# Weight sums of a block product: two of four made by accumulating loads, and the product's seven terms spread between other units

## What is computed

```python
def _swiglu(h, w_in, w_out):
    gu = h @ w_in
    gate, up = jnp.split(gu, 2, axis=-1)
    return (jax.nn.silu(gate) * up) @ w_out
...
    for l in range(DEPTH):
        x = x + 0.5 * _swiglu(_rmsnorm(x, ffn1_norm[l]), ffn1_w_in[l], ffn1_w_out[l])
        ...
        x = x + jnp.concatenate([out_a, out_b], axis=-1) @ w_mix_out[l]
        x = x + 0.5 * _swiglu(_rmsnorm(x, ffn2_norm[l]), ffn2_w_in[l], ffn2_w_out[l])
```

## Time and profile before

| what | us |
|---|---|
| median of 3 runs | 982.07 (978.37 to 983.84) |
| the profiled execution | 981.96 |
| its span, first to last instruction | 980.2 |
| TensorE busy | 902.0 |
| VectorE busy | 715.7 |
| ScalarE busy | 507.6 |

### The profile page before, as it was taken

How to read it: one execution, slowest core, us unless ns; L and a number is a source line. 1 busy time by engine, 2 the same in 40 slices (tenths; PEclk the granted TensorE clock), 3 DMA queues, 4 the chain that set the end, 5 groups by cost and what they waited for, 6 DMA issues and landing times.

```text
span 980.2 us, 10918 instructions
## 1 busy us (share of the span) xinstructions
PE 902.0 (92%) x4118; PEld 731.5 (75%) x4118; DVE 715.7 (73%) x857; ACT 507.6 (52%) x554; POOL 68.6 (7%) x123
## 2 busy tenths in 40 slices
...
GB/s 318 305 85 213 317 97 221 238 299 87 65 290 268 121 115 215 280 135 267 263 229 157 109 214 298 100 206 256 277 87 66 290 268 126 128 197 279 147 250 54
DMA packets 138467, 194.49 MB, mean 198 GB/s; under 512 B 9796, under 2 KB 94600, under 8 KB 138416
## 3 DMA queue, kind: packets, MB, share of 16 engines
q1 hardware_dynamic: 136432, 189.17, 58.2%
q0 software_dynamic: 1808, 4.49, 2.3%
...
...
## 4 chain that ended last, share of the span: by engine, by line
PE 40%; DVE 26%; DMA 17%; SPq 7%; ACT 6%; issue 3%; ACTq 0%; DVEq 0%
DVE w_lo L1093 13%; DMA h_rows<-qs 8%; DVE raw L1118 6%; DMA raw<-in_ffn_w_in_dram 5%; ACT w_hi L750 5%; PE U L1595 4%; PE U L1596 4%; PE U L1598 4%; SPq L470 4%; DMA gv<-h_rows 3%; PE C L1595 3%; PE C L1596 3%; PE C L1598 3%; PE TR L1595 3%; PE TR L1596 3%
## 5 line engine op out<-in xcount | busy, mean ns | idle before, releaser
L1093 DVE TENSOR_TENSOR w_lo<-raw,w_hi 128x2048 fp32r<-128x2048 f32 (+1 forms) x182 | 403.9, 2239 | 139.2 <-ACT w_hi L750 138.4
L750 ACT ACTIVATE w_hi<-raw 128x2048 fp32r<-128x2048 f32 (+1 forms) x178 | 333.2, 1891 | 208.0 <-DVE raw L1118 88.4
L1595 PE MATMUL U<-w_hi,xT 128*128 128x512 f32 (+1 forms) x352 | 137.6, 391 | 0.6 <-DVE xT L1261 0.6
L1596 PE MATMUL U<-w_lo,xT 128*128 128x512 f32 (+1 forms) x352 | 135.9, 386 | 0.0
L1598 PE MATMUL U<-w_hi,xT 128*128 128x512 f32 (+1 forms) x352 | 135.7, 386 | 0.0
L1595 PE MATMUL TR<-w_hi,xT 128*128 128x512 f32 x256 | 99.8, 390 | 0.0
L1598 PE MATMUL TR<-w_hi,xT 128*128 128x512 f32 x256 | 99.6, 389 | 0.0
L1596 PE MATMUL TR<-w_lo,xT 128*128 128x512 f32 x256 | 99.6, 389 | 0.0
L1595 PE MATMUL C<-w_hi,hT_hi 128*128 128x512 f32 x176 | 71.8, 408 | 15.0 <-DVE hT_lo L1175 15.0
L1595 PEld LDWEIGHTS U<-w_hi,xT 128*128 128x128 f32 x352 | 67.5, 192 | 14.3 <-DVE xT L1261 1.0
L1598 PEld LDWEIGHTS U<-w_hi,xT 128*128 128x128 f32 x352 | 67.5, 192 | 13.3
(11 more groups left out here) (206 smaller groups left out, 1269.5 us busy)
## 6 DMA issues: line engine op xcount, KB each, us to landing
raw<-in_ffn_w_in_dram SPq DMA_DIRECT2D x168, 512.0 KB, 6.3
raw<-in_ffn_w_out_dram SPq DMA_DIRECT2D x88, 512.0 KB, 6.3
raw<-in_w_mix_in_dram SPq DMA_DIRECT2D x28, 512.0 KB, 8.6
raw<-in_w_mix_out_dram SPq DMA_DIRECT2D x16, 512.0 KB, 4.0
...
xc<-bias_rows POOLq DMA_DIRECT2D x16, 192.0 KB, 6.4
```

The costliest lines, as they stand in the source:

```text
L750: return act.activation(w_hi[:, slot_of(u), cols], raw[:, raw_of(u), cols], ACT.Copy)
L1093: return dve.tensor_tensor(w_lo[:, slot_of(u), cols], raw[:, raw_of(u), cols], w_hi[:, slot_of(u), cols].bitcast(F32), ALU.subtract)
L1595: pe.matmul(out_, x_hi, w_hi[:, slot, c], start=start, stop=False, skip_group_check=reopened)
L1596: pe.matmul(out_, x_hi, w_lo[:, slot, c], start=False, stop=False, skip_group_check=reopened)
```

## The change

The seven terms are made and used in another order (B11, T1, T2, T3, B22, B21, T4), with units of `in` and `out` between them: `out` 1 or 4 and one unit of `in` c+2 come earlier, the pair's own `out`s later. T1 and T3 are no longer added by VectorE: GpSimd issues loads of B12 onto the slot that holds B11, and of B22 onto the slot of B12, that add to what is there (`accum_op`). VectorE keeps T2 and T4. B12 and B22 are still loaded plainly too. The trips of h, the banks and the raw slots follow the new order, and the end of the stage has `out` 7 and 8 around the transposes of chunk 10. ScalarE's order follows VectorE's and is left out below, as are the removed lists and the second pair's lines, which repeat the first's with 4 added to the chunks (`out` 4 in the place of `out` 1).

```diff
 OUT_TILES = (4, 6, 0, 2)
 QUADS = (3, 7)
 SINGLES = (0, 1, 2, 5, 6, 9, 10)
-TERMS = ("B11", "B21", "T1", "T2", "T3", "T4", "B22")
+TERMS = ("B11", "T1", "T2", "T3", "B22", "B21", "T4")
+FIRST_OUT = {3: 1, 7: 4}
 MIX = ("KV", "Q0", "Q1", "V0", "V1", "U0", "U1", "M0", "M1", "M2", "M3")
 LAYERS = 2
 
 
     def quad(c):
         term = {n: (s, "sum", c, n) for n in TERMS}
-        return [term["B11"], term["B21"], term["T1"], term["T2"], (s, "out", c - 1), term["T3"], term["T4"], term["B22"],
-                *inner(c + 2), (s, "out", c), (s, "out", c + 1), *inner(c + 3), (s, "out", c + 2)]
-
-    return [*inner(0), *inner(1), (s, "out", 0), *inner(2), (s, "out", 1), *quad(3), *quad(7), (s, "out", 10)]
+        return [term["B11"], (s, "out", FIRST_OUT[c]), term["T1"], (s, "in", c + 2, 0), term["T2"], (s, "out", c - 1), term["T3"],
+                (s, "in", c + 2, 1), term["B22"], term["B21"], term["T4"], (s, "in", c + 3, 0), (s, "out", c + 2),
+                (s, "in", c + 3, 1), (s, "out", c)]
+
+    return [*inner(0), *inner(1), (s, "out", 0), *inner(2), *quad(3), *quad(7), (s, "out", 8), (s, "out", 10)]
 
 
 def stage_used(s):
 
     made = stage_made(s)
-
-    def later(a, b):
-        made.remove(a)
-        made.insert(made.index(b) + 1, a)
-
     if s > 0:
-        later((s, "out", 0), (s, "in", 2, 0))
-    for c in QUADS:
-        later((s, "out", c - 1), (s, "sum", c, "T3"))
+        made.remove((s, "out", 0))
+        made.insert(made.index((s, "in", 2, 0)) + 1, (s, "out", 0))
     return made
 
...
     if u[1] != "sum":
         return [u]
-    return [(u[0], "sum", u[2], n) for n in ("B11", "B12", "B21", "B22")] if u[3] == "B11" else []
+    return [(u[0], "sum", u[2], n) for n in {"B11": ("B11",), "T1": ("B12",), "T2": ("B22",), "B21": ("B21",)}.get(u[3], ())]
 
 
...
 RAW_OF = {"B11": "B11", "B21": "B21", "B22": "B22", "T1": "B11", "T2": "B11", "T4": "B11", "T3": "B12"}
-HT_SLOT = {0: 0, 1: 1, 2: 0, 3: 0, 4: 1, 5: 0, 6: 1, 7: 0, 8: 1, 9: 1, 10: 0}
+HT_SLOT = {0: 0, 1: 1, 2: 0, 5: 1, 3: 0, 4: 1, 6: 0, 9: 1, 7: 0, 8: 1, 10: 0}
+HT_BEFORE = {5: 1, 6: 3, 9: 4, 3: 5, 7: 9}
 
 
...
     return [(c, t) for c in cs for t in range(2)]
 
 
-SILU_ORDER = counts(lambda s: [*both((0, 1, 2)), (3, 0), (3, 1), *both((5, 6)), (7, 0), (7, 1), *both((9, 10))])
-H_ORDER = counts(lambda s: [*both((0, 1, 2)), (3, 1), (3, 0), *both((5, 6)), (7, 1), (7, 0), *both((9, 10))])
+SILU_ORDER = counts(lambda s: both((0, 1, 2, 5, 3, 6, 9, 7, 10)))
+H_ORDER = SILU_ORDER
 HT_ORDER = H_ORDER
 HT_PSUM_ORDER = counts(lambda s: [(c, t) for c in (0, 10) if not by_trip(s, c) for t in range(2)])
-TRIP_ORDER = counts(lambda s: [(c,) for c in (0, 1, 2, 3, 5, 6, 7, 9) if by_trip(s, c)])
+TRIP_ORDER = counts(lambda s: [(c,) for c in (0, 1, 2, 5, 3, 6, 9, 7) if by_trip(s, c)])
 TRIP_B_ORDER = counts(lambda s: [(c,) for c in QUADS])
 GU_ORDER = counts(lambda s: [(c,) for c in SINGLES])
-ADD_ORDER = counts(lambda s: [(c, n) for c in QUADS for n in ("T1", "T3", "T2", "T4")])
+ADD_ORDER = counts(lambda s: [(c, n) for c in QUADS for n in ("T2", "T4")])
+SUM_LOAD_ORDER = counts(lambda s: [(c,) for c in QUADS])
 SNAP_ORDER = counts(lambda s: [(c, n) for c in QUADS for n in ("s1", "s2", "s3")])
-SUM_ORDER = counts(lambda s: [(c, n) for c in QUADS for n in ("gate0", "up1", "up0")])
+SUM_ORDER = counts(lambda s: [(c, n) for c in QUADS for n in ("up1", "up0", "gate0")])
 
 
...
 
     U = [bank("U0"), bank("U1")]
     TR = [bank("TR0"), bank("TR1")]
-    BANKS = {0: U, 1: TR, 2: U, 5: [TR[1], U[1]], 6: [U[0], TR[0]], 9: [TR[1], TR[0]], 10: U}
-    QUAD_BANKS = {3: (TR[0], TR[1], U[0]), 7: (U[1], TR[1], U[0])}
+    BANKS = {0: U, 1: TR, 2: U, 5: U, 6: [U[1], TR[1]], 9: [U[1], TR[1]], 10: [TR[1], U[0]]}
+    QUAD_BANKS = {3: (TR[0], U[0], TR[1]), 7: (TR[0], U[1], U[0])}
     acc = [[bank("C0"), bank("C1")], [bank("D0"), bank("D1")]]
...
+        load_block(s, 3, "B11")
         load_out(s, 1)
+        if by_trip(s, 0):
+            store_h(s, 0)
         load_block(s, 3, "B12")
         if by_trip(s, 0):
             load_h(s, 0)
+        load_in(s, 5, 0)
         store_h(s, 1)
         load_block(s, 3, "B22")
         load_h(s, 1)
         load_out(s, 2)
+        store_h(s, 2)
+        load_in(s, 5, 1)
+        load_h(s, 2)
+        load_block(s, 3, "B21")
+        load_in(s, 6, 0)
+        load_out(s, 5)
+        load_in(s, 6, 1)
+        load_out(s, 3)
+        store_h(s, 5)
+        load_block(s, 7, "B11")
+        load_h(s, 5)
+        load_out(s, 4)
+        store_g(s, 3)
+        load_block(s, 7, "B12")
+        store_h(s, 3)
+        load_g(s, 3)
+        load_h(s, 3)
+        load_in(s, 9, 0)
+        load_block(s, 7, "B22")
+        load_out(s, 6)
+        store_h(s, 6)
+        load_in(s, 9, 1)
+        load_h(s, 6)
+        load_block(s, 7, "B21")
+        load_in(s, 10, 0)
+        load_out(s, 9)
+        load_in(s, 10, 1)
+        load_out(s, 7)
+        store_h(s, 9)
+        load_out(s, 8)
+        load_h(s, 9)
+        load_out(s, 10)
+        store_g(s, 7)
+        store_h(s, 7)
+        load_g(s, 7)
+        load_h(s, 7)
+        if after is not None:
+            after()
 
     sp.dma_start(xs[:, 0, :], x_tiles[0]).then_inc(x_loaded[0], 16)
     load_first(0, 0)
...
         rsqrt(L, rstd[:, c0:c0 + groups], sums[:, c0:c0 + groups], mean[:, c0:c0 + groups], n,
               groups).then_inc(rstd_done, 1)
 
+    def add_block(s, c, to, name, landed_):
+
+        dst = raw[:, RAW_SLOT[s, "sum", c, to], :].rearrange("p (k n) -> p k n", k=4)
+        k0, col = 4 * (name[1] == "2"), DFF + c * FC
+        for i in range(2):
+            pool.dma_start(dst[:, 2 * i:2 * i + 2, :], w_in[s % 2][s // 2, :, k0 + 2 * i:k0 + 2 * i + 2, col:col + 2 * FC],
+                           accum_op=ALU.add).then_inc(landed_, 16)
+
+    def add_blocks(s, c):
+
+        r, n = landed((s, "sum", c, "B12"))
+        pool.wait_ge(unit_loaded[r], n)
+        add_block(s, c, "B12", "B22", T3_landed)
+        pool.wait_ge(lo_ready, n_made((s, "sum", c, "B11")))
+        add_block(s, c, "B11", "B12", T1_landed)
+
     inverse_rms(0, 0, 0)
     with nc.allow_non_contiguous_dma(reason="256 numbers, once"):
         pool.dma_start(rb[:, :], rel_bias.rearrange("b h -> h b")).then_inc(rb_loaded, 16)
...
     for j, u in enumerate([(s, "sum", 3, "B11"), (s, "sum", 3, "T2"), (s, "in", 5, 0), (s, "in", 6, 0)]):
         pool.wait_ge(units_used, n_used(u))
         pool.dma_start(ws[32 * j:32 * j + 32, :, :].rearrange("a g (i b) -> a (g i) b", b=32),
...
     if name[0] == "B":
         split(u)
         return
-    act.wait_ge(terms_added, ADD_ORDER[s, c, name])
+    if name == "T1":
+        act.wait_ge(T1_landed, 32 * SUM_LOAD_ORDER[s, c])
+    elif name == "T3":
+        act.wait_ge(T3_landed, 32 * SUM_LOAD_ORDER[s, c])
+    else:
+        act.wait_ge(terms_added, ADD_ORDER[s, c, name])
     hi_of(u).then_inc(hi_ready, 1)
 
...
             act.activation(s1, s1, ACT.Silu, scale=inv[:, 0:1]).then_inc(silu_done, 1)
         else:
             act.wait_ge(units_used, n_used((s, "sum", c, "T4")))
+            act.wait_ge(h_done, H_ORDER[s, c + 2, 1])
             act.activation(gate_pair, QUAD_BANKS[c][0][:, :], ACT.Silu, scale=inv[:, 1:2]).then_inc(silu_done, 1)
 
     def copy_sum(s, c, name):
...
+            act.wait_ge(units_used, n_used((s, "out", HT_BEFORE[c])))
         for kk in range(2):
             act.activation(h_as_tokens(hT_hi[:, HT_SLOT[c], kk, :]), h_as_loaded(h_cols, kk), ACT.Copy
                            ).then_inc(hT_hi_done, 1)
 
     def round_pair(s, c, t):
 
-        if t == 1:
+        if t == 0:
+            act.wait_ge(units_used, n_used((s, "out", HT_BEFORE[c])))
+            act.wait_ge(g_loaded, 64 * TRIP_B_ORDER[s, c])
+        else:
             act.wait_ge(h_loaded, 64 * TRIP_ORDER[s, c])
-        else:
-            act.wait_ge(g_loaded, 64 * TRIP_B_ORDER[s, c])
         act.activation(pair_as_tokens(hT_hi, t), pair_as_loaded(h_cols if t == 1 else g_cols), ACT.Copy
                        ).then_inc(hT_hi_done, 1)
...
 
     def add_term(s, c, name):
 
-        to, other = {"T1": ("B11", "B12"), "T2": ("B11", "B22"), "T3": ("B12", "B22"), "T4": ("B11", "B21")}[name]
+        to, other = {"T2": ("B11", "B22"), "T4": ("B11", "B21")}[name]
         r, n = landed((s, "sum", c, other))
         dve.wait_ge(unit_loaded[r], n)
-        if name == "T3":
-            r, n = landed((s, "sum", c, to))
-            dve.wait_ge(unit_loaded[r], n)
         a, b = [raw[:, RAW_SLOT[s, "sum", c, x_], :] for x_ in (to, other)]
         dve.tensor_tensor(a, a, b, ALU.add).then_inc(terms_added, 1)
 
...
+    combine_x(s)
+    term(3, "B11")
+    rest_h(s, 1)
     out(1)
+    rest_x(s)
+    multiply(s, 2, 0)
+    term(3, "T1")
+    add_term(s, 3, "T2")
+    multiply(s, 2, 1)
+    turn_h(s, 2)
+    made(5, 0)
+    term(3, "T2")
+    out(2)
+    rest_h(s, 2)
+    term(3, "T3")
+    add_term(s, 3, "T4")
+    made(5, 1)
+    term(3, "B22")
+    term(3, "B21")
```

(76 more changed lines are left out.)

224 lines of the change are left out of this document (92 added, 132 removed).

## The result

The changed kernel takes 1038.85 us in the median of 5 runs (1037.49 to 1044.71), against 982.07 before: a ratio of 1.0588 (95% interval 1.0549 to 1.0627), slower by 57 us. I had forecast 989 with a range to 1018. The chance for slower was 0.45, the largest of the three, but the size lies outside the range. The profiled execution took 1044.71 us, 5.9 above the median; its span is 1042.8 us and the mean granted clock 0.934 (0.963 before).

What follows compares the result with a forecast made beforehand. TensorE was taken to bound the kernel, with some 108 us lost to waits and slow clock. New losses of 90.4, 21 and 4 make 115.4 against 108, so +7: 989 us, range 955 to 1018.

Steps and rivals of the forecast that it cites:

- VectorE's sums: VectorE makes 16 sums fewer, 36.4 us less busy; time falls only where a wait is ordered behind them.
- The waits at out 5 and out 9: TensorE waits 4.1 us for rest_h at each, plus 1 us of slow clock, in every stage.
- No DMA can cure it: The out 5 and out 9 waits, in every stage, cannot be cured by any DMA.
- The end of the stage: Around the transposes of h: 0.5 us left a stage; the ends lose about 24 us now.
- Out 3: Second pair's T1 load lands late: 10.4 us wait, 1.5 of slow clock, a stage; clock counts from T3's product end.
- rival 1: Accumulating loads as cheap as plain ones: out 3 waits 3.7 us and 1 of slow clock, 960 us; chance 0.32.
- The rule of the Trainium skill: A DMA reduction is half as fast as a copy: two units 12.6 us, some 997 in all.
- The first pair: Waits at out 1 and in 5 with slow clock: 7 us in stages 1 to 3, 0 in stage 0.
- hidden but for this place: The 16.8 MB of added load traffic costs nothing except at out 3.
- Rival 2: Accumulating loads cost twice the software queue's price: 14.6 us more a stage, 1047 us; chance 0.13.
- Rival 3: VectorE runs far ahead, order-bound waits close; nearly all 108 us but first pair's and cheap out 3's go: about 930; chance 0.06.

Runs made afterwards that it cites:

- e8: e11 with the halves of out 1 and of T1 also put ahead of h of chunk 1; VectorE makes all four sums: 921.10 us.
- e12: e8 with T3 alone made by an accumulating load, issued once T1's sum has read B12: 922.69 us.
- e1: Changed kernel's new order, with VectorE making all sums and no GpSimd loads for the pairs: 993.38 us.
- e11: e1 with the first pair's rest_pair ahead of the second pair's T1 halves, and h of chunks 5 and 9 ahead of units queued in front: 946.92 us.
- e4: Changed kernel with round_pair and rest_pair of chunk 3 ahead of the second pair's T1 halves and T2 sum: 992.94 us.
- e3: Changed kernel with GpSimd's loads overwriting instead of adding, so T1 and T3 are B12 and B22 alone (a timing probe): 998.94 us.
- e2: Changed kernel with GpSimd issuing T1's accumulating load ahead of T3's: 1019.08 us.
- e9: e8's order with the changed kernel's accumulating loads, T1's issued first; T1's halves stay behind x_hi: 982.11 us.

## Why the prediction was wrong

**VectorE's sums: right.** It is 36.1 us less busy, and "no bound by throughput, only by order" holds: e8 has the work of before on VectorE and none of the waits for low halves of the earlier trace rows, and e12 has 8 sums fewer than e8 and is no faster.

**The waits at out 5 and out 9: right.** Forecast 4.1 us each, in every stage; the trace has 3.9 to 5.2 at the eight places, 4.11 at out 5 of stage 1. The clock after them costs more than the 1 us I gave (6.0 less 4.1 at out 5): behind the wait the starts lie up to 0.43 us apart until 417.4 us, where 1 us had stood for about five of them, and the granted clock of the stretch is 0.90. "No DMA can cure it" was right, too: L1231 is 38.2 us in e1, which has no such loads, against 40.0. What cured it was order (e11).

**The end of the stage: right.** No wait at the transposes is left in the table.

**Out 3: the mechanism was right and the size too small.** The step gave 11.9 us a stage; 18 are measured. T3's product ends at 388.16 us in TensorE's timeline of stage 1, so on the prediction's clock:

| step | forecast | measured |
|---|---|---|
| `turn_g(3)` ends | 17.2 | 18.7 |
| B12' landed | 24.3 | 27.3 |
| T1' landed | 38.3 | 44.3 |
| out 3 starts | 45.4 | 51.5 |

Each link is a little late. Landing took B12' 8.2 us and not 6.3; the DMA share of that stretch is 0.88, and that this is the reason is likely but not shown. From GpSimd's first issue to T1' there are 17.1 us and not 14: an addition costs 6.0 us a unit, not the 5.3 that I took from the nearest row, and GpSimd's issuing 1.2 us each (4.91 for four), not 0.6. e4 shows that this chain set the wait, since its move takes L1246 away.

Part of the nearness is luck. The 5.3 us a unit came from the other loads on the same queue and was taken for that queue's price, but plain loads of a unit cost 3.1 there (e3), the hardware queue's 3.16; it is the addition that makes 6.0. And at the plain price the step would have failed by more: rival 1 gave out 3 a loss of 4.7 us a stage, while e3, with that price, loses 11.7 there (12.5 in stage 0, 12.1 in stage 1).

The rule of the Trainium skill that I had weighed ("Collectives: The Full Stack", section "The bandwidth ceiling: the fold count and why AG ≠ RS ≠ AR"), half speed for a reduction, holds here in its number: 6.0 against 3.1 us a unit. Its reason, two reads for a sum, no run shows; the queue's packets are nearly twice as many with the addition. By it I had put 12.6 us for two units, near the 11.9 measured, but it would have moved the sum by 8 us only, to 997.

**The first pair: this step failed.** It said 7 us a stage and 0 in stage 0, "T1 of the first pair waits for no such load", and the added traffic "hidden but for this place". T1 indeed waits for none. But 47 us are lost there and not 21. The experiments, by the same measure over four stages:

| place | forecast | after | e1, no loads | e2, T1's first | e3, plain loads |
|---|---|---|---|---|---|
| first pair | 21 | 47 | 41 | 34 | 26 |
| out 5 | 20.4 | 26 | 25 | 26 | 26 |
| out 3 | 47.6 | 72 | 25 | 60 | 47 |
| out 9 | 20.4 | 27 | 27 | 29 | 28 |

Two things were wrong. The addition costs 21 us at the first pair (47 against 26 in e3), where the prediction had put it at nothing. And stage 0 was put at 0 for a reason of order that doesn't hold: with plain loads it loses 6.9 us, with none 7.8, and 16.1 in the kernel after. In stages 1 to 3 the 7 us were right for plain loads (6.0 to 6.5). e1's 41 us are another loss of the same size: there T1's half waits for VectorE's sum (13.2 us into TR), so the sums that were taken away did hold up T1.

How the addition reaches this place: out 1 waits 7.7 us in stage 0, and 23.5 in all, because ScalarE and VectorE take h of chunk 1 first, and h of chunk 1 comes late. In stage 0 SP issues its small loads right between GpSimd's; the timelines of GpSimd, SP and ScalarE in the kernel after:

```profile
36.65 2.53 POOL L706 DMA_DIRECT2D raw<-in_ffn_w_in_dram  x2 [7.04 <-DMA raw<-in_ffn_w_in_dram]
42.91 2.40 POOL L706 DMA_DIRECT2D raw<-in_ffn_w_in_dram  x2 [3.72 <-DVE w_lo L1158]
...
39.58 2.10 SPq L545 DMA_DIRECT2D gv<-h_rows  x4
...
55.01 0.72 ACT L865 ACTIVATE hT_hi<-gv 128x256 fp32r<-128x256 f32 x2 [17.67 <-DMA gv<-h_rows]
```

Issued by 41.7, four loads of 64 KB are there at 55.0: 13 us. SP issues them at the same time in e1 (39.62), e2 (39.79) and e3 (39.82). ScalarE takes the same h at 44.31 in e1 (no loads) and at 46.72 in e3 (loads without addition). In e2 GpSimd issues all its four loads from 43.25 on, too late to meet it, and ScalarE takes it at 44.24:

```profile
43.25 4.97 POOL L706 DMA_DIRECT2D raw<-in_ffn_w_in_dram  x4 [13.72 <-DVE w_lo L1158]
...
44.24 0.72 ACT L865 ACTIVATE hT_hi<-gv 128x256 fp32r<-128x256 f32 x2 [6.84 <-DMA gv<-h_rows]
```

Stage 1 shows it too: ScalarE takes h of chunk 1 at 355.77 us, 4.0 us behind the first pair product (351.81), and in e3 at 335.20, 0.15 ahead of it (335.35). The out 1 wait falls with it (L1158 into C from 23.5 to 3.9 us in e2's table, 4.1 in e3's). So it was accumulating loads in flight that held up this trip, in a place where nobody waits for the loads themselves. Rival 2 came near the time (1047), but by twice the software queue's price, all of it at out 3; neither was so. Rival 3's sum was also off: 982 less 108, with 21 for the first pair, 19 for the cheap out 3 and 6 for the rest put back, is 920 and not 930.

**In sum:** of 62 us unforeseen, 26 are the first pair, 24 out 3 and 12 the two `rest_h` places. By the experiments the 57 us are 11 of order (e1) and 45 of loads, 40 of them the addition (e3). The addition's share falls on the first pair (21) and on out 3 (25). The 5 us between e1 and e3 are a difference of two larger ones: 15 less at the first pair, where no sum holds up T1, and 22 more at out 3.

**Open.** Why 64 KB loads wait 13 us beside accumulating ones (which of the 16 DMA engines' queues held them) isn't settled. Nor was T1's load alone run in the best order. e12 can't say that T3's load is harmless in e9, since its place is another, behind the trip of h. Each kernel's losses by place are from one profiled execution.
